# Moving the low part of the inner features from VectorE to GpSimd in the seven-product pairs of a SwiGLU kernel

## The chip, the cores and the metric

The kernel runs on one core of one Trainium2 chip. The metric is the device time of one launch in microseconds, the median of several runs. TensorE (PE) does matmuls, VectorE (DVE) and ScalarE (ACT) elementwise work, GpSimd (POOL) here a few sums and some transfers, SyncE (SP) issues the weight loads.

## The reference, cut to what matters

The program is one step of a two-layer decoder trunk on 512 prompt positions and 32 sample positions (544 columns in all), width 1024. It has four SwiGLU channel mixers (FFNs), each with 2816 inner features:

```
def swiglu(x, w13, w2):
    gate, up = jnp.split(x @ w13, 2, axis=-1)
    return (jax.nn.silu(gate) * up) @ w2

x = layer_norm(ALPHA * x + 0.5 * swiglu(x, ffn_w13[layer, 0], ffn_w2[layer, 0]), ...)
x = layer_norm(ALPHA * x + mix, ...)            # pooling or dilated attention
x = layer_norm(ALPHA * x + 0.5 * swiglu(x, ffn_w13[layer, 1], ffn_w2[layer, 1]), ...)
```

Everything is in fp32. Each matmul is done in a faster format by splitting both factors into a high part (rounded to fp32r) and a low part (the rest), and adding three products: high x high, high x low, low x high.

## The kernel before, in words

Activations lie with features on the 128 partitions and the 544 columns along the free axis. An FFN's 2816 inner features are 22 units of 128; eleven of them are made in stage `up<f>a` and used in `down<f>a`, the other eleven in `up<f>b` and `down<f>b` (f is 0 to 3). The first units of an a stage (6 in `up0a`, 4 in each of the others, table `PLAIN`) are made plainly. The rest, 5, 7, 7 and 7 units of the a stages and all 11 of each b stage, 70 in all, are made as "seven-product pairs": gate and up product of one unit are computed together from seven products of quarter matrices, after sums and differences of the weight quarters. A pair is 7 x 12 = 84 matmuls on TensorE.

What follows is what each engine does for one pair `i`, in the order of its program; the order is written out by hand in one function `pair` per engine.

- SP (`stream_seven`) loads four quarters of the raw weights of the next unit, each when the piece of `raw` has been read: quarters 0 and 2 first, quarter 1, and quarter 3 last, once `seven_low(5)` has read the old one.
- ACT (`pair`, L1444) rounds the seven weight quarters or sums (`seven_high`, tiles `t_a_hi`, `t_s_hi`, `t_w_seven`), takes the silu in two halves, copies one product (`t_p`), and rounds the finished features of the unit before (`hidden_hi`, tile `t_h_hi`, L1412).
- DVE (`pair`, L1947) makes the sums of the weight quarters for the next unit (`w_sums`, tile `t_w_sum`, L1922), the low parts of the seven (`seven_low`, L1927), combines the products (`added`, tiles `t_u` and `t_c`, L1931), multiplies silu and up part into `hf` in two halves (`hidden_seven`, L1943), and makes the low part of the features of the unit before: `hidden_lo`, L1873 to L1877, tile `t_h_lo`, hf minus its rounded part, 128 x 544.
- PE (`pair`, L881) does product 0 to 6. Product 6 adds to the bank from which DVE has just made `c22`, so it waits for that (`pe.wait_ge(c_made, 5 * y + 3)`).

`hf` is one buffer: `hidden_seven(stage, i, 0)` waits for `h_lo_made` of the unit before. PE waits for `h_lo_made` once more: in the first turn of `down`, which follows the last pair, for the last but one unit at k = 0 and for the last unit at k = 10 of 11 (`each`, L961).

GpSimd in this kernel: after each FFN and mixer, `sums` (L2439, tensor_tensor adds of 128 x 544, L2449 and L2451, beside a stage whose DVE work is `residual` and `round_lo`, L1805) and `centre` (L2457, L2463, 128 x 272), between `down2b` and `wo` the loads of the caches and small copies. In the FFNs before `down<f>b` it waits.

Of the kernel before, what the change touches and what calls it, by code (L numbers as in the profile page):

```python
# [24 lines left out]
F32 = mybir.dt.float32  # L25
F32R = mybir.dt.float32r
ACT = mybir.ActivationFunctionType
ALU = mybir.AluOpType
# [45 lines left out]
PLAIN = {"up0a": 6, "up1a": 4, "up2a": 4, "up3a": 4, "up0b": 0, "up1b": 0, "up2b": 0, "up3b": 0}  # L74
# [19 lines left out]
UNITS = {n: u for n, u, _ in STAGES}  # L94
# [9 lines left out]
HIDDEN = {n: FC * int(n[2]) + (KH if n[3] == "b" else 0) for n in PLAIN}  # L104
# [51 lines left out]
def first_turn(i):  # L156
    return isinstance(i, int) and i == 0
# [26 lines left out]
def build(nc, A, O):  # L184
# [3 lines left out]
    def sb(where, name, shape, dt=F32):  # L188
        return where.enter_context(nc.sbuf_tensor("t_" + name, shape, dt))

    def sem(name):
        return ctx.enter_context(nc.semaphore(name))

    with ctx:
# [23 lines left out]
        sg, hf, sq = (elem[:, j * T:(j + 1) * T] for j in range(3))  # L218
# [35 lines left out]
        hhi = sb(rh, "h_hi", [P, KH, T], F32R)  # L254
        hlo = sb(rh, "h_lo", [P, KH, T], F32R)
# [99 lines left out]
        def hcols(j):  # L355
            return slice(j * HALF, (j + 1) * HALF)
# [57 lines left out]
        h_hi_made = sem("hidden_hi_made")  # L414
        h_lo_made = sem("hidden_lo_made")
# [1373 lines left out]
        def _(dve):  # L1789
# [57 lines left out]
            n = NBUCKET + 1  # L1847
# [25 lines left out]
            def hidden_lo(stage, i):  # L1873
                dve.wait_ge(h_hi_made, HIDDEN[stage] + i + 1)
                one = lambda t: t.rearrange("p (a n) -> p a n", a=1)
                nc.vector.tensor_tensor(hlo[:, bass.ds(i, 1), :], one(hf[:]), hhi[:, bass.ds(i, 1), :].bitcast(F32),
                                        ALU.subtract).then_inc(h_lo_made, 1)  # L1877
# [27 lines left out]
            def w_sums(y, m):  # L1905
                if m == 0:
                    dve.wait_ge(quarter_in[3], 16 * (y + 1))
                    a, b, op = quarter(2), quarter(3), ALU.add
                elif m == 1:
                    dve.wait_ge(w_sum_made, 4 * y + 2)  # L1910
                    a, b, op = w_sum[0][:], quarter(0), ALU.subtract
                elif m == 2:
                    dve.wait_ge(quarter_in[0], 16 * (y + 1))
                    dve.wait_ge(quarter_in[2], 16 * (y + 1))
                    if not (isinstance(y, int) and y == 0):
                        dve.wait_ge(seven_lo_made, 7 * y - 3)
                    a, b, op = quarter(0), quarter(2), ALU.subtract
                else:
                    dve.wait_ge(quarter_in[1], 16 * (y + 1))
                    dve.wait_ge(w_sum_made, 4 * y + 3)  # L1920
                    a, b, op = quarter(1), w_sum[1][:], ALU.subtract
                nc.vector.tensor_tensor(w_sum[m][:], a, b, op).then_inc(w_sum_made, 1)  # L1922

            def seven_low(n, y):
                src = (quarter(0), w_sum[1][:], w_sum[0][:], w_sum[2][:], quarter(1), quarter(3), w_sum[3][:])[n]
                dve.wait_ge(seven_hi_made, 7 * y + n + 1)
                nc.vector.tensor_tensor(seven_lo[n][:], src, seven_hi[n][:].bitcast(F32), ALU.subtract) \  # L1927
                    .then_inc(seven_lo_made, 1)

            def added(out, a, b):  # L1930
                nc.vector.tensor_tensor(out[:], a, b[:], ALU.add).then_inc(c_made, 1)  # L1931

            def c_last(y, odd):
                dve.wait_ge(seven_done, 7 * y + 7)
                added(c12, pb[:, odd, 0:HALF], u2)

            def hidden_seven(stage, i, half):
                y = SEVEN[stage] + i - PLAIN[stage]
                dve.wait_ge(seven_silu, 2 * y + 1 + half)
                if half == 0:  # L1940
                    dve.wait_ge(h_lo_made, HIDDEN[stage] + i)
                    dve.wait_ge(c_made, 5 * y + 4)
                m = nc.vector.tensor_tensor(hf[:, hcols(half)], sg[:, hcols(half)], (c21, c22)[half][:], ALU.mult)  # L1943
                if half:
                    m.then_inc(h_made, 1)

            def pair(stage, i, odd):  # L1947
                y = SEVEN[stage] + i - PLAIN[stage]
                first = isinstance(i, int) and i == PLAIN[stage]
                last = isinstance(i, int) and i == UNITS[stage] - 1  # L1950
                if not first:
                    c_last(y - 1, 1 - odd)
                seven_low(6, y)
                if not first:
                    hidden_seven(stage, i - 1, 1)
                if not last:
                    seven_low(0, y + 1)
                if not first:
                    hidden_lo(stage, i - 1)
                if not last:  # L1960
                    w_sums(y + 1, 2)
                    w_sums(y + 1, 0)
                dve.wait_ge(p1_copied, y + 1)
                dve.wait_ge(seven_done, 7 * y + 2)
                added(u2, pc[:, 0, 0:HALF], p1)
                if not last:
                    w_sums(y + 1, 1)
                    w_sums(y + 1, 3)
                    seven_low(1, y + 1)
                    seven_low(2, y + 1)  # L1970
                dve.wait_ge(seven_done, 7 * y + 4)
                dve.wait_ge(c_made, 5 * y + 1)
                added(u3, pc[:, 1, 0:HALF], u2)
                dve.wait_ge(c_made, 5 * y + 2)
                added(c22, pb[:, odd, 0:HALF], u3)
                if not last:
                    seven_low(3, y + 1)
                    seven_low(4, y + 1)
                if last:
                    round_lo(AFTER[stage], 0, 0)  # L1980
                dve.wait_ge(seven_done, 7 * y + 6)
                added(c21, pd[:, 0, 0:HALF], u3)
                hidden_seven(stage, i, 0)
                if not last:
                    seven_low(5, y + 1)
                    return
                c_last(y, odd)
                hidden_seven(stage, i, 1)
                round_lo(AFTER[stage], 1, 0)
                hidden_lo(stage, i)  # L1990

            def pairs(stage):
                n = PLAIN[stage]
# [442 lines left out]

        @block.gpsimd
        def _(pool):
            def sums(stage):  # L2439

                pool.wait_ge(res_made, RBASE[stage] + 1)
                nc.gpsimd.memset(accs[:], 0.0).then_inc(acc_zero, 1)  # L2442
                nc.gpsimd.memset(accq[:], 0.0).then_inc(acc_zero, 1)
                pool.wait_ge(acc_zero, 2 * RES.index(stage) + 2)
                def add(c):
                    if not first_turn(c):
                        pool.wait_ge(acc_made, ABASE[stage] + 2 * c)
                    pool.wait_ge(res_made, RBASE[stage] + c + 1)
                    nc.gpsimd.tensor_tensor(accs[:], accs[:], x[:, c, :], ALU.add).then_inc(acc_made, 1)  # L2449
                    pool.wait_ge(sq_made, RBASE[stage] + c + 1)  # L2450
                    nc.gpsimd.tensor_tensor(accq[:], accq[:], sq[:], ALU.add).then_inc(acc_made, 1)  # L2451

                add(0)
                with pool.Fori(1, DC - 2) as c:
                    add(c)

            def centre(stage):  # L2457

                n = RES.index(stage)
                for j in range(2):  # L2460
                    pool.wait_ge(ln_std, 2 * n + j + 1)
                    for c in range(5, DC):
                        nc.gpsimd.tensor_tensor(x[:, c, hcols(j)], x[:, c, hcols(j)], mean[:, hcols(j)], ALU.subtract) \  # L2463
                            .then_inc(ln_sub, 1)

            sums("down0b")
            centre("down0b")

            pool.wait_ge(utok_ok, 1)
            pool.dma_start(O["pool_p"][0, 0, :, :], utok[0:PAD, :]).then_inc(utok_out, 16)  # L2470
            pool.dma_start(O["pool_s"][0, :, PAD - DEC_S:PAD, :], utok[PAD:PAD + SAMP, :]).then_inc(utok_out, 16)
            sums("pout")
            centre("pout")
            sums("down1b")
            centre("down1b")

            sums("down2b")
            centre("down2b")

# [80 lines left out]
            pool.wait_ge(o_ready, GC)  # L2560
            sums("wo")
            centre("wo")
            sums("down3b")
            centre("down3b")

# [22 lines left out]
```

## Time and profile before

| | us |
|---|---|
| median of 3 runs (lowest, highest) | 2268.6 (2266.86, 2274.68) |
| the profiled execution | 2272.91 |
| its span | 2271.2 |
| TensorE busy in the span | 2154.2 (95%) |
| VectorE busy | 1443.8 (64%) |
| ScalarE busy | 867.1 (38%) |
| GpSimd busy | 224.5 (10%) |

The span runs from the first to the last instruction; the 1.7 us between it and the execution's own time are around it. Busy shares are averages over stages of very different kinds, and matmuls overlap one another, so that a gap of under 0.16 us between two matmul starts doesn't show as idle time of TensorE. For a stage, the starts of instructions in a timeline tell more.

### The profile page before, as it was taken

The numbers are of one execution on the slowest core, as the hardware profiler recorded it, in microseconds if no ns is written. First come the engines' busy times: TensorE is split into PE (matmuls) and PEld (weight loads), VectorE is DVE, ScalarE is ACT, GpSimd is POOL, SyncE is SP. The second block draws the span as 40 slices with busy tenths as digits, with TensorE's granted clock in tenths as the row PEclk, the third lists the DMA queues.
The fourth block names the chain that finished last, engine by engine and source line by source line (L and its number), as shares of the span: only waits on it lengthen the run. The fifth ranks groups of instructions, "written<-read, shape, count | busy, mean of one in ns | idle before, by whom it ended". The sixth has DMA issues, their size and how long they took to land.

```text
span 2271.2 us, 44028 instructions
## 1 busy us (share of the span) xinstructions
PE 2154.2 (95%) x16591; PEld 2056.9 (91%) x16591; DVE 1443.8 (64%) x2474; ACT 867.1 (38%) x1521; POOL 224.5 (10%) x240
## 2 busy tenths in 40 slices
PE   7999999979999999999999999989889988999998
PEld 7899999969999999999999999988856688999997
DVE  3582894684894696479469652467444376937955
ACT  3341453442552344355235434222222345514533
POOL 0000002204000001300000130210020040000022
PEclk9999999989999999999999999999877889999998
DMA  4242433212233233234333324666663322333331
GB/s 136 73 132 85 128 112 103 67 52 80 76 100 94 86 93 101 76 95 142 102 94 97 100 79 156 210 211 214 200 209 115 111 75 70 92 95 89 95 106 53
DMA packets 381501, 249.78 MB, mean 110 GB/s; under 512 B 10423, under 2 KB 363039, under 8 KB 381327
## 3 DMA queue, kind: packets, MB, share of 16 engines
q1 hardware_dynamic: 371271, 210.00, 31.2%
q0 software_dynamic: 10096, 37.94, 4.8%
q8 instruction: 91, 1.49, 0.3%
q14 instruction: 43, 0.34, 0.1%
HBM read 230.63 MB, written 22.35 MB: 111 GB/s over the span
## 4 chain that ended last, share of the span: by engine, by line
PE 74%; DVE 11%; DMA 6%; issue 4%; ACT 3%; SPq 1%; POOL 1%; DVEq 0%; ACTq 0%; POOLq 0%
PE pair L748 33%; PE pair L877 25%; PE pair L787 5%; DMA t_w_raw<-in_attn_w_kv 3%; PE pair L1005 2%; DMA t_w_raw<-in_ffn_w 2%; PE pair L1239 2%; DVE t_w_seven L1927 2%; PE pair L1156 1%; DVE t_w_sum L1922 1%; PE pair L1262 1%; PE pair L760 1%; DVE t_w_lo L1805 1%; ACT t_w_hi L1362 1%; DVE t_u_sum L2214 1%
## 5 line engine op out<-in xcount | busy, mean ns | idle before, releaser
L877 PE MATMUL pair<-t_x_diff_hi,t_w_seven 128*128 128x272 f32 x1960 | 410.0, 290 | 0.0
L1362 ACT ACTIVATE t_w_hi<-t_w_raw 128x1024 fp32r<-128x1024 f32 (+2 forms) x152 | 177.1, 1170 | 465.0 <-PE pair L748 389.8
L1805 DVE TENSOR_TENSOR t_w_lo<-t_w_raw,t_w_hi 128x1024 fp32r<-128x1024 f32 (+2 forms) x152 | 232.6, 1531 | 190.9 <-ACT t_w_hi L1362 185.4
L877 PEld LDWEIGHTS pair<-t_x_diff_hi,t_w_seven 128*128 128x128 f32 x1960 | 320.6, 188 | 0.0
L748 PE MATMUL pair<-t_h_lo,t_w_hi 128*128 128x272 f32 x1232 | 255.2, 288 | 0.0
L748 PE MATMUL pair<-t_h_hi,t_w_lo 128*128 128x272 f32 x1232 | 255.0, 288 | 0.0
L877 PE MATMUL pair<-t_x_hi,t_w_seven 128*128 128x272 f32 x1120 | 240.9, 295 | 14.8 <-DVE t_c L1931 13.2
L748 PE MATMUL pair<-t_h_hi,t_w_hi 128*128 128x272 f32 x1232 | 254.8, 288 | 0.0
L877 PE MATMUL pair<-t_x_diff_lo,t_w_seven 128*128 128x272 f32 x840 | 241.9, 288 | 0.0
L877 PEld LDWEIGHTS pair<-t_x_hi,t_w_seven 128*128 128x128 f32 x1120 | 184.6, 188 | 27.1 <-issue 12.8
L748 PEld LDWEIGHTS pair<-t_h_hi,t_w_lo 128*128 128x128 f32 x1232 | 193.2, 188 | 0.0
L748 PEld LDWEIGHTS pair<-t_h_hi,t_w_hi 128*128 128x128 f32 x1232 | 193.2, 188 | 0.0
L748 PEld LDWEIGHTS pair<-t_h_lo,t_w_hi 128*128 128x128 f32 x1232 | 193.1, 188 | 0.0
L1433 ACT ACTIVATE t_w_seven<-t_w_sum 128x512 fp32r<-128x512 f32 x210 | 124.6, 622 | 113.0 <-PE pair L877 79.6
L877 PE MATMUL pair<-t_x_lo,t_w_seven 128*128 128x272 f32 x560 | 161.8, 289 | 0.0
L877 PEld LDWEIGHTS pair<-t_x_diff_lo,t_w_seven 128*128 128x128 f32 x840 | 158.7, 189 | 0.0
L1927 DVE TENSOR_TENSOR t_w_seven<-t_w_sum,t_w_seven 128x512 fp32r<-128x512 f32 x210 | 143.5, 683 | 0.2
L748 PE MATMUL pair<-t_x_hi,t_w_hi 128*128 128x272 f32 x576 | 124.2, 298 | 20.3 <-DVE t_w_lo L1805 15.7
L2442 POOL MEMSET t_work<- 128x544 f32 x6 | 3.3, 553 | 1403.1 <-DVE t_stream L2075 1403.1
L1433 ACT ACTIVATE t_s_hi<-t_w_sum 128x512 fp32r<-128x512 f32 x70 | 44.3, 633 | 247.3 <-DVE t_w_sum L1922 222.9
L748 PE MATMUL pair<-t_x_lo,t_w_hi 128*128 128x272 f32 x576 | 122.6, 295 | 0.0
L748 PE MATMUL pair<-t_x_hi,t_w_lo 128*128 128x272 f32 x576 | 122.4, 295 | 0.0
(308 smaller groups left out, 5046.3 us busy)
## 6 DMA issues: line engine op xcount, KB each, us to landing
t_w_raw<-in_ffn_w SPq DMA_DIRECT2D x280, 256.0 KB, 3.1
t_w_raw<-in_ffn_w SPq DMA_DIRECT2D x64, 704.0 KB, 4.5
t_w_raw<-in_ffn_w SPq DMA_DIRECT2D x36, 512.0 KB, 3.8
t_cached<-in_cache_kv_w POOLq DMA_DIRECT2D x16, 1024.0 KB, 9.0
t_cached_v<-in_cache_kv_w POOLq DMA_DIRECT2D x16, 1024.0 KB, 10.3
t_w_raw<-in_attn_w_kv SPq DMA_DIRECT2D x24, 512.0 KB, 8.0
t_w_raw<-in_attn_w_q SPq DMA_DIRECT2D x12, 512.0 KB, 3.8
scratch_bias_rows<-scratch_bias_row SPq DMA_DIRECT2D x12, 384.0 KB
```

Source lines behind the costliest of these rows:

```text
L748: m = nc.tensor.matmul(out[:, j, 0:HALF], w[:, at + k, :], a(k)[:, j * HALF:(j + 1) * HALF], start=first and k == 0 and n == 0, stop=last ...
L760: return nc.tensor.matmul(out[:, j, 0:HALF], invd[:], a[:, hcols(j)], start=first, stop=not first)
L787: m = nc.tensor.matmul(ps[2 * u + s][:, j, 0:HALF], w[:, k, :], a[:, k, hcols(j)], start=k == 0 and n == 0, stop=k == DC - 1 and n == 2)
L877: m = nc.tensor.matmul(out[:, 0:HALF], w[:, k, :], b, start=start and k == 0 and j == 0, stop=k == 3 and j == 2, skip_group_check=not start)
L1005: m = nc.tensor.matmul(ps[s][:, j, 0:HALF], w[:, k, :], a(k)[:, hcols(j)], start=k == 0 and n == 0, stop=k == KT[stage] - 1 and n == 2)
L1156: nc.tensor.matmul(out[:, (g + 1) * P:(g + 2) * P], q_r[hd, g * GC + c, :], k_r[hd, (g - 1) * GC + c, :], start=True, stop=True)
L1239: m = nc.tensor.matmul(pd[32 * s:32 * s + 32, 0, :], p_b[s][:, t, :], v_c0[s][:] if t == 0 else v_c[s][:, t - 1, :], start=t == 0, stop=t ...
L1262: m = nc.tensor.transpose(pb[:, h % 2, k * P:(k + 1) * P], p_p[h % 2][:, k * P:(k + 1) * P], ident[:])
L1362: nc.scalar.activation(whi[s][:, 0:KT[stage], :], raw[s][:, 0:KT[stage], :], ACT.Copy) \
L1433: nc.scalar.activation(seven_hi[n][:], src, ACT.Copy).then_inc(seven_hi_made, 1)
L1805: nc.vector.tensor_tensor(wlo[s][:, 0:k, :], raw[s][:, 0:k, :], whi[s][:, 0:k, :].bitcast(F32), ALU.subtract).then_inc(lo_made[s], 1)
L1927: nc.vector.tensor_tensor(seven_lo[n][:], src, seven_hi[n][:].bitcast(F32), ALU.subtract) \
```

## The change

For the 70 seven-product pairs `hidden_lo` is made by GpSimd. It has a loop for each of the eight up stages, placed in its program ahead of the sums of that FFN. Each turn waits until ACT has rounded unit i, subtracts, and raises `h_lo_made` as DVE did. DVE drops the instruction and its wait from `pair`; it still makes `hidden_lo` for the 18 plain units.

```
@@ DVE, pair
                 if not last:
                     seven_low(0, y + 1)
-                if not first:
-                    hidden_lo(stage, i - 1)
                 if not last:
                     w_sums(y + 1, 2)
                     w_sums(y + 1, 0)
...
                 hidden_seven(stage, i, 1)
                 round_lo(AFTER[stage], 1, 0)
-                hidden_lo(stage, i)
@@ GpSimd
+            def hidden_lo(stage):
+                one = hf[:].rearrange("p (a n) -> p a n", a=1)
+                with pool.Fori(PLAIN[stage], UNITS[stage]) as i:
+                    pool.wait_ge(h_hi_made, HIDDEN[stage] + i + 1)
+                    nc.gpsimd.tensor_tensor(hlo[:, bass.ds(i, 1), :], one, hhi[:, bass.ds(i, 1), :].bitcast(F32),
+                                            ALU.subtract).then_inc(h_lo_made, 1)
...
+            hidden_lo("up0a")
+            hidden_lo("up0b")
             sums("down0b")
             centre("down0b")
```

The same two calls stand ahead of `sums("down1b")`, `sums("down2b")` and `sums("down3b")`.

On DVE, in the loop of the pairs, these rows stood from the low part of quarter a11 to the second sum (`t_a_lo` is `seven_low(0)`, `t_w_sum` are `w_sums` 2 and 0, `t_u` the first addition of products):

```order
L1927 TENSOR_TENSOR t_a_lo<-t_w_raw,t_a_hi 128x512 [waits seven_hi_made]
L1874 REGISTER_ALU
L1876 ISA [waits hidden_hi_made]
L1876 TENSOR_TENSOR t_h_lo<-t_elementwise,t_h_hi 128x544
L1913 ISA
L1916 REGISTER_ALU [waits w_quarter_in2,w_quarter_in0]
L1922 TENSOR_TENSOR t_w_sum<-t_w_raw 128x512 [waits seven_lo_made]
L1922 TENSOR_TENSOR t_w_sum<-t_w_raw 128x512 [waits w_quarter_in3]
```

and now:

```order
L1927 TENSOR_TENSOR t_a_lo<-t_w_raw,t_a_hi 128x512 [waits seven_hi_made]
L1913 ISA
L1916 REGISTER_ALU [waits w_quarter_in2,w_quarter_in0]
L1922 TENSOR_TENSOR t_w_sum<-t_w_raw 128x512 [waits seven_lo_made]
L1922 TENSOR_TENSOR t_w_sum<-t_w_raw 128x512 [waits w_quarter_in3]
L1962 REGISTER_ALU [waits p1_copied]
L1931 TENSOR_TENSOR t_u<-pair,t_p 128x272 [waits seven_products]
```

The subtraction and its wait for ACT are gone, and the two sums stand directly behind `t_a_lo`.

GpSimd's program now begins, behind its constants, with the loops of `up0a` and `up0b`:

```order
L2438 UNCONDITIONAL_BRANCH
L2438 ISA
L2440 ISA [waits hidden_hi_made]
L2440 ISA
L2440 TENSOR_TENSOR t_h_lo<-t_elementwise,t_h_hi 128x544
L2438 REGISTER_ALU
L2438 COMPARE_AND_BRANCH
```

One wait and one subtraction per turn; before, the first rows behind the constants were the memsets of `sums("down0b")`. The rows of PE and ACT are the same in both kernels.

## Rows read from the trace of the kernel before

**Rows 1.** The page's busy time, share of the span and instructions of each engine.

```profile
PE 2154.2 (95%) x16591; PEld 2056.9 (91%) x16591; DVE 1443.8 (64%) x2474; ACT 867.1 (38%) x1521; POOL 224.5 (10%) x240
```

**Rows 2.** Engines' busy time in stretches of pairs; columns in the first line.

```profile
core 0: us, PE busy (x) PEld busy (x) DVE busy (x) ACT busy (x) POOL busy (x), PEclk, DMA share, GB/s
268.47:333.62 65.15, 64.95 (x507) 63.69 (x505) 61.48 (x115) 33.78 (x66) 0.00 (x0) 1.00 0.39 116
...
635.33:645.97 10.64, 10.64 (x86) 10.61 (x85) 10.16 (x19) 5.54 (x11) 0.00 (x0) 1.00 0.35 101
```

**Rows 3.** Timeline of PE around product 6; start, length, what.

```profile
310.00 0.29 PE L877 MATMUL pair<-t_x_diff_hi,t_w_seven 128*128 128x272 f32 x1
310.32 0.39 PE L877 MATMUL pair<-t_x_hi,t_w_seven 128*128 128x272 f32 x1
310.55 0.29 PE L877 MATMUL pair<-t_x_lo,t_w_seven 128*128 128x272 f32 x1
```

**Rows 4.** Timeline of DVE in that pair; in brackets idle time and who ended it.

```profile
303.44 0.69 DVE L1927 TENSOR_TENSOR t_a_lo<-t_w_raw,t_a_hi 128x512 fp32r<-128x512 f32 x1 [0.18 <-ACT t_a_hi L1433]
304.42 0.73 DVE L1876 TENSOR_TENSOR t_h_lo<-t_elementwise,t_h_hi 128x544 f32 x1 [0.29 <-ACT t_h_hi L1412]
305.06 1.29 DVE L1922 TENSOR_TENSOR t_w_sum<-t_w_raw 128x512 f32<-128x512 f32 x2
306.26 0.43 DVE L1931 TENSOR_TENSOR t_u<-pair,t_p 128x272 f32<-128x272 f32 x1
...
309.75 0.44 DVE L1931 TENSOR_TENSOR t_c<-pair,t_u 128x272 f32<-128x272 f32 x1
```

**Rows 5.** Timeline of ACT in that pair.

```profile
303.58 0.65 ACT L1412 ACTIVATE t_h_hi<-t_elementwise 128x544 f32 x1
```

**Rows 6.** The load of quarter 3 in that pair: SP's timeline, then the DMA view.

```profile
302.12 0.37 SPq L572 DMA_DIRECT2D t_w_raw<-in_ffn_w  x1
...
t_w_raw<-in_ffn_w SPq DMA_DIRECT2D x1, 256.0 KB, 3.0
```

**Rows 7.** Timeline of POOL, then of DVE, in `down0b`.

```profile
381.14 1.36 POOL L2449 TENSOR_TENSOR t_work<-t_work,t_stream 128x544 f32<-128x544 f32 x1 [4.37 <-DVE t_stream L2075]
382.45 2.75 POOL L2451 TENSOR_TENSOR t_work<-t_work,t_elementwise 128x544 f32<-128x544 f32 x1
...
381.52 2.46 DVE L1805 TENSOR_TENSOR t_w_lo<-t_w_raw,t_w_hi 128x1408 fp32r<-128x1408 f32 x1 [0.56 <-ACT t_w_hi L1362]
```

**Rows 8.** Timeline of POOL, then of DVE, in a `centre`.

```profile
434.54 1.83 POOL L2463 TENSOR_TENSOR t_stream<-t_stream,t_work 128x272 f32<-128x272 f32 x1 [13.65 <-ACT t_work L1561]
...
434.52 1.22 DVE L1802 TENSOR_TENSOR t_w_lo_second<-t_w_raw,t_w_hi_second 128x1024 fp32r<-128x1024 f32 x1
435.65 1.85 DVE L2125 RECIPROCAL t_work<-t_work 128x272 f32<-128x272 f32 x1
```

**Rows 9.** POOL, whole run: `centre` in ns min/median/max; a group with a cast.

```profile
L2463 POOL TENSOR_TENSOR t_stream<-t_stream,t_work x36: 755/772/1835, 418.6 to 2258.1; 128x272 f32<-128x272 f32 x36
L2498 POOL CAST t_one_hot<-t_ident_twice 64x512 fp32r (+1 forms) x8 | 4.9, 608 | 116.6 <-DVE t_k_times_q L2270 116.5
```

**Rows 10.** Timeline of DVE in the second pair of `up0b`.

```profile
249.04 0.69 DVE L1927 TENSOR_TENSOR t_a_lo<-t_w_raw,t_a_hi 128x512 fp32r<-128x512 f32 x1 [0.68 <-ACT t_a_hi L1433]
249.88 0.73 DVE L1876 TENSOR_TENSOR t_h_lo<-t_elementwise,t_h_hi 128x544 fp32r<-128x544 f32 x1
```

**Rows 11.** Timeline of DVE in a pair of `up1b`.

```profile
805.18 0.69 DVE L1922 TENSOR_TENSOR t_w_sum<-t_w_raw 128x512 f32<-128x512 f32 x1
806.32 0.69 DVE L1922 TENSOR_TENSOR t_w_sum<-t_w_raw 128x512 f32<-128x512 f32 x1 [0.44 <-DMA t_w_raw<-in_ffn_w]
```

**Rows 12.** End of `up0b`: timeline of DVE, then the chain that ended last.

```profile
356.54 1.62 DVE L1805 TENSOR_TENSOR t_w_lo<-t_w_raw,t_w_hi 128x1408 fp32r<-128x1408 f32 x1
358.07 0.72 DVE L1876 TENSOR_TENSOR t_h_lo<-t_elementwise,t_h_hi 128x544 fp32r<-128x544 f32 x1
...
355.20 49.77 PE pair L748 x396
```

More of the change, by code:

```diff
@@ L1957, in pair @@
                     seven_low(0, y + 1)
-                if not first:
-                    hidden_lo(stage, i - 1)
                 if not last:
@@ L1989, in pair @@
                 round_lo(AFTER[stage], 1, 0)
-                hidden_lo(stage, i)
             def pairs(stage):
@@ L2438, in _, with hidden_lo @@
         def _(pool):
+            def hidden_lo(stage):
+                one = hf[:].rearrange("p (a n) -> p a n", a=1)
+                with pool.Fori(PLAIN[stage], UNITS[stage]) as i:
+                    pool.wait_ge(h_hi_made, HIDDEN[stage] + i + 1)
+                    nc.gpsimd.tensor_tensor(hlo[:, bass.ds(i, 1), :], one, hhi[:, bass.ds(i, 1), :].bitcast(F32),
+                                            ALU.subtract).then_inc(h_lo_made, 1)
             def sums(stage):
@@ L2464, in centre @@
                             .then_inc(ln_sub, 1)
+            hidden_lo("up0a")
+            hidden_lo("up0b")
             sums("down0b")
@@ L2473, in _ @@
             centre("pout")
+            hidden_lo("up1a")
+            hidden_lo("up1b")
             sums("down1b")
             centre("down1b")
+            hidden_lo("up2a")
+            hidden_lo("up2b")
             sums("down2b")
@@ L2562, in _ @@
             centre("wo")
+            hidden_lo("up3a")
+            hidden_lo("up3b")
             sums("down3b")
```

## The prediction

> **What bounds the kernel now.** The page comes first. TensorE is busy 95% of the span, VectorE 64%, GpSimd 10% [rows 1]. That average says that DVE has room, and it is the wrong place to stop, because the change touches only the seven-product pairs. So the next view is the busy time by stretch, laid over the pairs. Six pairs of `up0b` take 65.15 us, 10.86 each, and in them DVE is busy 61.48, 10.25 per pair [rows 2]: 94%, not 64%. PE shows 64.95 busy in the same stretch, but its matmuls overlap, so I ask the timeline for their starts. They come every 0.12 to 0.13 us, except at product 6: 310.00 to 310.32, then 310.55 [rows 3], that is 0.19 + 0.10 = 0.29 us lost. Product 6 waits for `c22`, and DVE ends that `t_c` at 309.75 + 0.44 = 310.19 [rows 4]. So in these pairs PE waits for DVE, hidden below the threshold at which idle time shows. What PE could do without this: a pair that lost almost nothing took 10.64 [rows 2], and 396 matmuls of a down stage took 49.77 us, 0.1257 each, which gives 84 x 0.1257 = 10.56 for a pair [rows 12]. PE's floor is then 10.56 to 10.64, and 0.22 to 0.30 us per pair could be had from a faster DVE.
>
> In one turn DVE waits for no matmul. It runs from sum to sum, and waits only for ACT: 0.18 before `t_a_lo` and 0.29 before `t_h_lo` [rows 4]. Hence DVE's own chain of instructions is the period of the pair, and whatever it gains or loses, the pair gains or loses, down to PE's floor.
>
> **How many pairs.** There are 70. In the first pair of each of the 8 stages nothing was moved, and the last pair is treated below. 70 - 16 = 54 pairs are left.
>
> **What the change removes from DVE.** `t_a_lo` starts at 303.44 and is followed by a 0.69 us instruction; behind such a one the next starts 0.60 later (two `t_w_sum` take 1.29, so the second starts 0.60 after the first [rows 4]). Without `t_h_lo` the first sum can start at 304.04 in place of 305.06: 1.02 us earlier, 0.64 of it the instruction and 0.38 the wait for ACT.
>
> **What it adds.** On its own engine, nothing that matters: GpSimd is idle here, its subtraction of 128 x 544 should take what its additions of that size take when nothing disturbs them, 1.36 us [rows 7], and `hf` is needed again only by `hidden_seven`, which stands behind `c22` (309.75 [rows 4]), over 5 us later. The question is what it does to DVE. In `down0b` the two engines meet [rows 7]. DVE's `t_w_lo` of 1408 columns starts at 381.52 while GpSimd's first addition runs to 382.50, and takes 2.46 us in place of 1.62 (its length undisturbed [rows 12]). It ends at 383.98 as if it had begun at 382.36, 0.14 before GpSimd's end. GpSimd's second addition, issued at 382.45, takes 2.75 in place of 1.36: it ends at 385.20, 1.22 after DVE's end. So each of the two waits for the other's whole instruction when both read two operands from SBUF. `centre` says the same: GpSimd's instruction of 272 columns takes 0.77 as a rule [rows 9], and 1.83 when it meets a 1.22 us one of DVE [rows 8]; it ends at 436.37, 0.63 after DVE's 435.74, and 0.77 - 0.14 is 0.63. The reciprocal behind it, with one operand, starts at 435.65 while GpSimd works and takes its 1.85 [rows 8].
>
> Now the same in a pair. ACT ends `t_h_hi` at 303.58 + 0.65 = 304.23 [rows 5]. DVE took 0.19 from there to start [rows 4], so I let GpSimd ask at 304.42. DVE is then in its first sum, 304.04 to 304.73, two operands from SBUF: GpSimd waits. The second sum could start at 304.64, but it needs quarter 3, whose load was issued at 302.12 and takes 3.0 to land [rows 6], 305.1. So nobody contests GpSimd's turn. It ends at 304.73 + 1.22 = 305.95, and DVE's second sum begins in effect at 305.95 - 0.14 = 305.81. Before, it began at 305.06 + 0.60 = 305.66. **The pair becomes 0.15 longer, not shorter**: 1.02 us are taken off DVE, the early quarter is not there to use them, and the port costs 1.17 from the end of the first sum (1.22 - 0.14 + the 0.09 by which two instructions overlap). Both engines' orders behind it are unchanged, so the shift runs through to `c22` and PE. The same reckoning on the other steady pairs gives 0.15 to 0.17; I take 0.16.
>
> Seven pairs, the second of a stage, differ: there `t_h_lo` follows `t_a_lo` by 0.84 in place of 0.98 [rows 10], since ACT was early. Less wait is removed, and they lose 0.30 each. In three pairs the second sum waited for its quarter well past the subtraction (805.18 + 0.60 = 805.78, started 806.32 [rows 11]); GpSimd's turn fits into that wait but for some 0.04.
>
> Sum: 44 x 0.16 + 7 x 0.30 + 3 x 0.04 = 7.0 + 2.1 + 0.1 = **9.2 us slower**.
>
> **Costed at nothing.** The last pair: PE's first down turn asks for the last unit's `t_h_lo` at k = 10, after 60 matmuls, 355.20 + 7.5 = 362.7. GpSimd asks at about 357.5, waits for `t_w_lo` (to 358.16 [rows 12]) and ends 1.22 later, 359.4. The cover is 3.3 us; if GpSimd needed more, PE would wait at 8 places. The other `t_h_lo` of the last pair lies beside DVE's wait for PE. The loops stand ahead of `sums`, which can't start before the down stage has its first result; no transfer of GpSimd is passed.
>
> **Bounds of the unknown.** No row has a GpSimd two-operand instruction that writes fp32r. From below: if its output cost nothing and it were no obstacle at all, DVE would gain 0.46 (the sum at 305.2, when the quarter lands) and PE's floor caps that at 0.28, 54 x 0.28 = 15 us gained. From above: add a whole cast to fp32r, 0.61 [rows 9]: 54 x 0.61 = 33 more. I take the plain 1.36, the nearest row.
>
> The Trainium skill, GPSIMD Engine Reference, § Performance versus the Vector engine, gives 4497 ns for a two-input add of 2048 fp32 columns. By length alone that is an estimate of 1.19 us for 544 columns; the sum would be 54 x 0.17 lower, 0 in place of 9. The trace has 1.36 for this size and that is what I use.
>
> **The rivals.**
> 1. *PE becomes the bound* (faster). If GpSimd gets its operands beside DVE's instructions, or in DVE's pauses, DVE's chain falls below PE's floor and each pair takes 10.58: -15 us, 2254. The reciprocal above was not held up, and `t_u`, 128 x 272, reads only one operand from SBUF: a turn of GpSimd that began under it would hide 0.36 us of its hold. Against it: GpSimd asks before the first sum ends, and the turn then falls at once. The Trainium skill, SBUF — State Buffer, § Who interferes with whom, has the rule: a DVE instruction with at most one SBUF input doesn't contend, one with two does. By that rule the sums contend, and the trace agrees with 2.46 in place of 1.62.
> 2. *A draw.* Turns shorter by 0.1 to 0.2 than the additions', or a part of the gained 1.02 kept elsewhere (ACT's `t_s_hi`, the loads): the two sides cancel, 0 to +5, about 2271.
> 3. *A dearer turn.* The fp32r output makes the instruction 0.3 longer, or DVE and GpSimd meet twice in a pair: +0.3 x 54 = 16 on top of 9, 2294.
> 4. *It doesn't do what it says*: GpSimd's loops would have to be late for `hidden_seven`. With 5 us to spare I give that no chance of its own.
>
> **How the numbers follow.** The profiled execution took 2272.9 in all (span 2271.2); with 9.2 it would take 2282.1. It lies 4.3 above the median of the runs shown, and the same 9.2 on 2268.6 gives 2277.8, so 2278. Chances: forecast 0.62, rival 1 0.12, rival 2 0.13, rival 3 0.13. 0.3% (what a measurement can tell from no change) is 6.8 us. The forecast's own range is +6 to +13, and I give a tenth of it to "same": slower 0.56 + 0.13 = 0.69, same 0.19, faster 0.12. The range leaves out rival 1's centre and the far half of rival 3: 2263 to 2290.
>
> **What would show it.** `t_h_lo` on GpSimd at about 1.5 us each in the pairs (1.36 and a short wait). In a steady pair DVE's second sum should be recorded with some 1.3 us in place of 0.69, all other DVE instructions unchanged. Six pairs in place of 65.15 should take 66.1, and the gap before product 6 should grow by 0.16. Down stages, norms and attention must be unchanged to 1 us in all. I am wrong if the pairs take 10.6 (no lock), if a sum shows 0.69 beside a running GpSimd instruction, or if the turn is much over 1.5 us.

## The result and the profile after

The changed kernel takes 2277.18 us (median of 20 runs, 2268.65 to 2287.23), the kernel before 2267.3 (20 runs, 2259.01 to 2276.48). The ratio is 1.0039, with a 95% interval of 1.0027 to 1.0051: 8.8 us slower, between 6.1 and 11.6. Forecast were 9.2.

The profiled executions alone would mislead: the span after is 2267.1 us, 4.1 shorter than before's 2271.2. So the first thing to do is to cut both at the pairs. These are the stretches of before, then of after, up to the first pair of `up0a`, and from the last pair of `up2b` to the first of `up3a` (columns as in [rows 2]):

```profile
0.00:111.61 111.61, 97.16 (x656) 90.97 (x656) 48.45 (x66) 34.81 (x45) 0.20 (x4) 0.95 0.36 102
1268.83:1914.67 645.84, 599.01 (x4671) 532.36 (x4669) 333.68 (x606) 212.50 (x389) 104.47 (x154) 0.90 0.47 150
```

```profile
0.00:107.02 107.02, 92.90 (x655) 87.65 (x656) 48.36 (x66) 34.84 (x45) 0.20 (x4) 0.98 0.36 106
1268.25:1908.85 640.60, 596.45 (x4671) 529.74 (x4669) 332.54 (x604) 212.70 (x389) 107.86 (x156) 0.91 0.47 151
```

4.6 and 5.2 us were gained, the first where no instruction was changed, the second where only the two subtractions at the last pair of `up2b` were moved. The column PEclk, the share of full speed that TensorE was granted, differs in both: 0.95 and 0.98 in the first stretch, 0.90 and 0.91 in the second. Length times missing share gives, as an estimate, 5.6 us lost to the clock in the first stretch before and 2.1 after, so most of the 4.6. The runs of one kernel scatter by more than this (2259 to 2276), which is why 20 runs of each are compared. In the pairs, where the granted clock is 1.00 in every stretch of both kernels, the picture is another. This is the sum row over eight stretches, each from the second pair of a stage to its last, 54 pairs, of before and then of after:

```profile
sum 589.66, PE 583.93 PEld 573.37 DVE 554.18 ACT 302.56 POOL 0.00; mean PE 72.99 PEld 71.67 DVE 69.27 ACT 37.82 POOL 0.00
```

```profile
sum 596.92, PE 584.78 PEld 573.32 DVE 553.12 ACT 302.46 POOL 82.35; mean PE 73.10 PEld 71.66 DVE 69.14 ACT 37.81 POOL 10.29
```

7.3 us longer. TensorE's and ScalarE's busy time stayed. DVE's fell by only 1.1, although 54 instructions of 0.73 were taken from it: most of that came back as longer instructions, for a held instruction is recorded with its wait. The steady pairs, answering to [rows 2]:

```profile
264.11:330.22 66.11, 64.97 (x506) 63.70 (x505) 62.07 (x109) 33.77 (x66) 9.17 (x6) 1.00 0.38 115
632.06:642.99 10.93, 10.83 (x86) 10.61 (x85) 10.12 (x18) 5.53 (x11) 1.50 (x1) 1.00 0.35 99
```

Six pairs take 66.11 in place of 65.15, and the second pair of `up1a` 10.93 in place of 10.64. In the timelines of DVE and of POOL, answering to [rows 4], one sees where:

```profile
299.52 0.69 DVE L1927 TENSOR_TENSOR t_a_lo<-t_w_raw,t_a_hi 128x512 fp32r<-128x512 f32 x1 [0.16 <-ACT t_a_hi L1433]
300.13 0.68 DVE L1922 TENSOR_TENSOR t_w_sum<-t_w_raw 128x512 f32<-128x512 f32 x1
301.31 1.28 DVE L1922 TENSOR_TENSOR t_w_sum<-t_w_raw 128x512 f32<-128x512 f32 x1 [0.49 <-DMA t_w_raw<-in_ffn_w]
302.51 0.43 DVE L1931 TENSOR_TENSOR t_u<-pair,t_p 128x272 f32<-128x272 f32 x1
```

```profile
300.51 1.53 POOL L2440 TENSOR_TENSOR t_h_lo<-t_elementwise,t_h_hi 128x544 f32 x1 [9.48 <-ACT t_h_hi L1412]
```

GpSimd asks at 300.51 while the first sum runs to 300.81, ends at 302.04, 1.23 after it, and the second sum takes 1.28 in place of 0.69: its end, 302.59, is that of an instruction begun at 301.90, 0.14 before GpSimd's. Part of the hold lies under the 0.49 us in which DVE waits for quarter 3 anyway. Product 6 then waits longer than in [rows 3], 0.48 from one start to the next in place of 0.32:

```profile
306.09 0.29 PE L877 MATMUL pair<-t_x_diff_hi,t_w_seven 128*128 128x272 f32 x1
306.57 0.39 PE L877 MATMUL pair<-t_x_hi,t_w_seven 128*128 128x272 f32 x1 [0.19 <-DVE t_c L1931]
306.80 0.29 PE L877 MATMUL pair<-t_x_lo,t_w_seven 128*128 128x272 f32 x1
```

### The profile page after: what moved, and what is told of

The parts are those of the page before. It is cut to its first block, busy times and chain, and to the rows that moved or that the text cites. A ratio compares the mean times of both kernels' runs of the same rounds, so it can differ in the third digit from the quotient of the medians.

```text
span 2267.1 us, 44233 instructions
## 1 busy us (share of the span) xinstructions
PE 2147.8 (95%) x16591; PEld 2049.9 (90%) x16591; DVE 1432.9 (63%) x2404; ACT 867.4 (38%) x1521; POOL 332.8 (15%) x310
## 4 chain that ended last, share of the span: by engine, by line
PE 62%; DVE 16%; DMA 9%; issue 7%; ACT 3%; SPq 1%; POOL 1%; DVEq 0%; ACTq 0%; POOLq 0%
PE pair L748 33%; PE pair L877 13%; DMA t_w_raw<-in_ffn_w 6%; PE pair L787 5%; DVE t_w_seven L1927 4%; DMA t_w_raw<-in_attn_w_kv 3%; PE pair L1005 2%; PE pair L1239 2%; DVE t_w_sum L1922 2%; DVE t_u L1931 2%; DVE t_c L1931 1%; PE pair L1156 1%; PE pair L1262 1%; PE pair L760 1%; DVE t_w_lo L1805 1%
## 5 line engine op out<-in xcount | busy, mean ns | idle before, releaser
L2440 POOL TENSOR_TENSOR t_h_lo<-t_elementwise,t_h_hi 128x544 f32 x70 | 108.1, 1544 | 1195.2 <-ACT t_h_hi L1412 1195.2
L1922 DVE TENSOR_TENSOR t_w_sum<-t_w_raw 128x512 f32<-128x512 f32 x140 | 129.6, 928 | 57.8 <-DMA t_w_raw<-in_ffn_w 57.8
```

The lines of the kernel that those rows point to most:

```text
L2440: nc.gpsimd.tensor_tensor(hlo[:, bass.ds(i, 1), :], one, hhi[:, bass.ds(i, 1), :].bitcast(F32), ALU.subtract).then_inc(h_lo_made, 1)
```

## The experiments

The edits are shown against the changed kernel where nothing else is said. Each ratio is against runs of the kernel before that were made beside it: 25 runs with a median of 2267.57 us for the first four experiments, 21 runs with 2265.39 for the other four. "54 pairs" is the sum over the same eight stretches as above, 589.66 before. The theory under test is that of the prediction: an instruction of DVE and one of GpSimd that read through the same port wait for each other's full length, and what that costs depends on what DVE has to do just then. The rivals are that DVE's removed microsecond was of no use to begin with, and that GpSimd's turn has a fixed price wherever it stands.

**Take the reading away.** The subtraction becomes a memset, so the low part of these features is left out.

```
-                with pool.Fori(PLAIN[stage], UNITS[stage]) as i:
+                for i in range(PLAIN[stage], UNITS[stage]):
                     pool.wait_ge(h_hi_made, HIDDEN[stage] + i + 1)
-                    nc.gpsimd.tensor_tensor(hlo[...], one, hhi[...].bitcast(F32), ALU.subtract).then_inc(h_lo_made, 1)
+                    nc.gpsimd.memset(hlo[:, bass.ds(i, 1), :].bitcast(F32), 0.0).then_inc(h_lo_made, 1)
```

> GpSimd's 70 subtractions of the pairs are replaced by memsets of 128x544 that write zeros into t_h_lo and read nothing; the low part of those features is left out of the result. DVE's program is that of the changed kernel. Theory (each engine waits for the other's whole instruction when both read two operands from SBUF): DVE's second t_w_sum is no longer held (0.69 us, not 1.3) and starts when quarter 3 lands, about 0.46 us earlier than in the kernel before; DVE's chain falls under PE's floor, a steady pair takes 10.56 to 10.64 in place of 10.86, and the whole is 12 to 15 us faster than before (ratio 0.9935 to 0.995). Rival A (DVE's removed microsecond is not usable at all, because the quarters or ACT set the chain): pairs stay at 10.86, ratio 1.000. Rival B (the price of GpSimd's turn is its semaphores and its start, not the port): pairs stay at 11.02, ratio 1.004.

Measured: ratio 0.9938 (0.9921 to 0.9956), 14 us faster than before (9 runs). DVE and POOL in a pair of `up1a`:

```profile
667.63 0.69 DVE L1927 TENSOR_TENSOR t_a_lo<-t_w_raw,t_a_hi 128x512 fp32r<-128x512 f32 x1 [0.46 <-ACT t_a_hi L1433]
668.24 1.29 DVE L1922 TENSOR_TENSOR t_w_sum<-t_w_raw 128x512 f32<-128x512 f32 x2
```

```profile
668.48 0.55 POOL L2440 MEMSET t_h_lo<- 128x544 f32 x1 [10.01 <-ACT t_h_hi L1412]
```

Two sums in 1.29 us as before, with a memset of GpSimd running beside them; all 70 memsets take 0.551 to 0.557. The pairs of this stage take 10.57, PE's floor: the stretch of five reads

```profile
633.56:686.39 52.83, 52.83 (x422) 52.83 (x421) 49.03 (x92) 28.38 (x55) 2.77 (x5) 1.00 0.31 91
```

Rivals A and B both fall: the microsecond is usable (54 pairs in 575.22), and neither the semaphores nor the start of GpSimd's instruction is what costs. One detail was not as expected. DVE's second sum doesn't stand at the landing of the quarter here. Once PE is the bound, DVE waits earlier (0.46 us before `t_a_lo`), and the quarter has landed by then.

**Two halves, each where it is covered.** Nothing is left out.

```
+                def turn(i, placed):
                     pool.wait_ge(h_hi_made, HIDDEN[stage] + i + 1)
...
+                    half(0, h_lo_half)
+                    pool.wait_ge(h_lo_half, SEVEN[stage] + i - PLAIN[stage] + 1)
+                    if placed:
+                        pool.wait_ge(seven_lo_made, 7 * (SEVEN[stage] + i - PLAIN[stage] + 2) + 2)
+                    half(1, h_lo_made)
```

`half(j, ...)` is the same subtraction on half `j` of the columns, 0 to 271 or 272 to 543; `placed` is false for the last two units of a stage.

> Nothing is left out. GpSimd makes t_h_lo in two halves of 128x272: the first as soon as ACT has rounded the unit, the second when DVE has made the second low part of the next pair (seven_lo_made), so that it lies under t_u and t_c, which have only one operand in SBUF; in the last two units of a stage it doesn't wait. Theory (the port is held for the instruction's length, and only against DVE instructions with two SBUF operands): the first half asks at 304.4, runs from the end of the first t_w_sum (304.73) to 305.36 and is out of the way at 305.22, just when quarter 3 has landed (305.1 to 305.2); the second is held from 309.4 to 309.9 under 0.82 us of t_u and t_c. Both are free, a steady pair takes PE's 10.56 to 10.64, 12 to 15 us faster than before (ratio 0.9935 to 0.995). Rival (a GpSimd instruction costs DVE a fixed price wherever it stands): two instructions per pair cost at least what one did, 11.02 or more per pair, ratio 1.004 or more.

Measured: ratio 0.996 (0.9943 to 0.9977), 9 us faster (9 runs), 54 pairs in 577.81. The second half, DVE and then POOL:

```profile
666.68 0.68 DVE L1928 TENSOR_TENSOR t_w_seven<-t_w_sum,t_w_seven 128x512 fp32r<-128x512 f32 x1
667.28 0.43 DVE L1932 TENSOR_TENSOR t_u<-pair,t_u 128x272 f32<-128x272 f32 x1
667.74 0.44 DVE L1932 TENSOR_TENSOR t_c<-pair,t_u 128x272 f32<-128x272 f32 x1
668.10 0.68 DVE L1928 TENSOR_TENSOR t_w_seven<-t_w_sum,t_w_seven 128x512 fp32r<-128x512 f32 x1
```

```profile
666.95 1.05 POOL L2442 TENSOR_TENSOR t_h_lo<-t_elementwise,t_h_hi 128x272 f32 x1 [3.16 <-DVE t_w_seven L1928]
```

GpSimd waits for the low part (ends 667.36) and is done at 668.00. `t_u` and `t_c`, whose other operand comes from PSUM, run beside it at their usual length, and the next low part, begun at 668.10, is not held. The fixed-price rival, 1.004 or more, falls. The first half is not free of DVE as expected: in the next pair of `up1a` it asks at 673.41, and the second sum, ready at 673.95, takes 0.95 in place of 0.69. That costs nothing where PE is the bound. The pairs of `up1a` stand at 10.57, but those in the first part of `up0b` do not, and the whole fell short of the 12 to 15 us: see the experiment with the bias pieces.

**One instruction, later.** The whole subtraction, behind the same wait for DVE.

```
+                def turn(i, placed):
                     pool.wait_ge(h_hi_made, HIDDEN[stage] + i + 1)
+                    if placed:
+                        pool.wait_ge(seven_lo_made, 7 * (SEVEN[stage] + i - PLAIN[stage] + 2) + 2)
                     nc.gpsimd.tensor_tensor(hlo[...], one, hhi[...].bitcast(F32), ALU.subtract).then_inc(h_lo_made, 1)
```

> Nothing is left out. GpSimd makes t_h_lo in one instruction of 128x544, but only when DVE has made the second low part of the next pair, so that it begins under t_u and t_c. Theory: 1.17 us of hold less the 0.82 us of t_u and t_c leave 0.35 for the next low part (recorded near 1.0 us in place of 0.68); the second t_w_sum comes 0.46 us earlier than before. Net 0.11 us less per pair than before: 10.75, and 6 us faster in all (ratio 0.997). Rival (position doesn't matter, only the amount): 11.02 per pair, ratio 1.004.

Measured: ratio 0.9975 (0.996 to 0.9989), 5.7 us faster (12 runs); the median of the 54 pair periods is 10.70. The low part behind `t_c` is held, DVE then POOL:

```profile
668.88 0.44 DVE L1932 TENSOR_TENSOR t_c<-pair,t_u 128x272 f32<-128x272 f32 x1
669.24 1.03 DVE L1928 TENSOR_TENSOR t_w_seven<-t_w_sum,t_w_seven 128x512 fp32r<-128x512 f32 x1
```

```profile
668.08 1.63 POOL L2443 TENSOR_TENSOR t_h_lo<-t_elementwise,t_h_hi 128x544 f32 x1 [9.09 <-DVE t_w_seven L1928]
```

1.03 against 0.68, that is the 0.35 expected. It is the same in all eight stages: beside GpSimd's subtraction all 54 `t_u` take 0.43 and all 54 `t_c` 0.44, and the low part behind them 1.01 to 1.04. The rival that these two are spared for being short (272 columns), and not for their operand in PSUM, doesn't fit another row: in the changed kernel DVE's `t_stream` of 128 x 544, which also reads PSUM, runs from 1821.15 to 1821.87 beside two additions of GpSimd (1820.12 to 1821.47, 1821.44 to 1822.80), takes its usual 0.72 and holds neither. The same instruction, elsewhere, turns 8.8 us of loss into 5.7 of gain: place decides, not amount.

**Twice.** GpSimd subtracts twice for every unit.

```
-                with pool.Fori(PLAIN[stage], UNITS[stage]) as i:
+                for i in range(PLAIN[stage], UNITS[stage]):
                     pool.wait_ge(h_hi_made, HIDDEN[stage] + i + 1)
+                    nc.gpsimd.tensor_tensor(hlo[...], one, hhi[...].bitcast(F32), ALU.subtract).then_inc(h_lo_half, 1)
+                    pool.wait_ge(h_lo_half, SEVEN[stage] + i - PLAIN[stage] + 1)
                     nc.gpsimd.tensor_tensor(hlo[...], one, hhi[...].bitcast(F32), ALU.subtract).then_inc(h_lo_made, 1)
```

> GpSimd subtracts twice for every unit of a pair, one after the other; the result is unchanged. Theory: the second turn asks at 306.2, during DVE's second t_w_sum (ends 306.5), and ends at 307.7; 0.36 of its hold lies under t_u, so the third t_w_sum is held by some 0.8 us. Steady pair 11.8, the whole 9 + 54 x 0.8 = 52 us slower than before (ratio 1.023). If only the quarter's wait made the first turn costly, or DVE had slack left, the second would cost little: under 0.3 per pair, ratio under 1.011.

Measured: ratio 1.024 (1.021 to 1.0269), 54 us slower (two runs). DVE, then POOL:

```profile
310.20 0.43 DVE L1932 TENSOR_TENSOR t_u<-pair,t_p 128x272 f32<-128x272 f32 x1
310.55 1.50 DVE L1923 TENSOR_TENSOR t_w_sum<-t_w_sum,t_w_raw 128x512 f32<-128x512 f32 x1
```

```profile
309.81 1.69 POOL L2444 TENSOR_TENSOR t_h_lo<-t_elementwise,t_h_hi 128x544 fp32r<-128x544 f32 x1
```

The third sum is held by 1.50 - 0.68 = 0.82, and the pairs take 71.04 / 6 = 11.84:

```profile
269.32:340.36 71.04, 64.97 (x507) 63.70 (x505) 66.83 (x109) 33.09 (x66) 20.02 (x12) 1.00 0.35 106
```

DVE has no slack in a pair of this kernel: the hold of 0.82 comes back whole in the period, 11.84 against 11.02.

**One operand on GpSimd.** A copy of `hf` in place of the subtraction, so the low part of these features is not made.

```
-                    nc.gpsimd.tensor_tensor(hlo[...], one, hhi[...].bitcast(F32), ALU.subtract).then_inc(h_lo_made, 1)
+                    nc.gpsimd.tensor_copy(hlo[:, bass.ds(i, 1), :], one).then_inc(h_lo_made, 1)
```

> GpSimd's subtraction is replaced by a copy of hf (128x544) into t_h_lo, one operand read from SBUF; so the low part is wrong in the result. Theory in its strict form (GpSimd's reads go through the port that DVE's second operand needs): the copy, alone some 0.65 us (a cast of 64x512 took 0.61), asks at 304.4 while DVE's first t_w_sum runs to 304.73, waits for it, is recorded with about 0.8 and is over by 305.3, under the wait for quarter 3; pairs take 10.57 as with the memset and the ratio is 0.994. Rival (only two-operand instructions of GpSimd take part): it is recorded with its own length in every pair, none longer by 0.1 or more; the pairs are the same.

Measured: ratio 0.9945 (0.9927 to 0.9962), 12.5 us faster (two runs). DVE, then POOL:

```profile
665.24 1.73 DVE L1922 TENSOR_TENSOR t_w_sum<-t_w_raw 128x512 f32<-128x512 f32 x2
```

```profile
665.59 0.84 POOL L2440 CAST t_h_lo<-t_elementwise 128x544 f32 x1 [9.73 <-ACT t_h_hi L1412]
```

The copy's shortest record in the run is 0.643; here it takes 0.84, because it waits for the first sum, and the two sums take 1.73 in place of 1.29. So a GpSimd instruction with one operand takes part too, and the rival falls. The total doesn't show it, since these pairs are bound by PE. One step was off: the copy was to be over before quarter 3 lands, but here the second sum is held by 0.44.

**Only the last unit of a stage on GpSimd.** One part of the change alone.

```
@@ DVE, pair
+                if not first:
+                    hidden_lo(stage, i - 1)
@@ GpSimd
-                with pool.Fori(PLAIN[stage], UNITS[stage]) as i:
+                for i in (UNITS[stage] - 1,):
```

> DVE makes t_h_lo in all pairs as before, and GpSimd only that of the last unit of each stage (8 in place of 70 instructions). Theory: its turn ends some 3 us before PE needs it, and nothing changes: steady pairs 10.86, ratio 1.000 within 0.002. Rival (part of the loss is at the ends of the stages, where PE or the next stage's DVE work waits for GpSimd): ratio 1.002 or more, and PE shows a gap at k = 10 of the first down turn.

Measured: ratio 1.0004 (0.9988 to 1.002; 10 runs). The ends of the stages cost nothing that this resolves, as forecast. In `down0b` GpSimd's turn ends at 355.27, PE asks for its result some 60 matmuls behind 350.94, at about 358.5, and its matmuls go on there at 0.125 us each, without a gap. The 54 pairs, whose program is that of before, summed to 588.42 in this execution, 1.2 less than before's 589.66, so such a sum scatters by at least that. One pair makes up 0.74 of it: the fourth of `up3a`, in which DVE waits for a weight quarter, took 12.24 before and 11.50 here, and 11.50 to 12.46 over all ten traces.

**The pieces of the bias table moved.** Against the kernel with the placed halves: SP sends the pieces elsewhere.

```
-            stream_all("down0a")
-            for i in range(7):
-                stream_seven("up0b", i)
+            for i in range(4):
+                stream("down0a", i)
                 bias_piece(1 if i < 3 else 2, (i + 1) % 4)
-            stream_all("up0b", 7)
+            stream_all("up0b")
...
+            for i in range(4):
+                stream("down0b", i)
+                if i < 3:
+                    bias_piece(2, i + 1)
```

> The kernel with two placed halves, and the seven pieces of the bias table (384 KB each) that SP sends during the first seven pairs of up0b are sent during down0a (4) and down0b (3). Nothing is left out. Theory: in up0b the pairs that stay at 10.86 with the halves and with the memset are bound by the landing of the weight quarters beside these pieces, not by DVE; they now take 10.57 like the others, 7 x 0.29 = 2 us less, and the down stages have room for the pieces (5.6 MB in 66 us). Ratio to before 0.994. Rival (these pairs are slow for another reason, a chain of DVE and ACT that starts late in this stage): they stay at 10.86 and the ratio at 0.996.

Measured: ratio 0.9944 (0.9925 to 0.9963), 12.7 us faster than before (6 runs), the lowest ratio of the versions that leave nothing out. The nine middle pairs of `up0b`, with the halves alone and then with the pieces moved:

```profile
243.68:341.36 97.68, 96.67 (x758) 95.39 (x757) 88.78 (x163) 51.10 (x99) 17.83 (x18) 1.00 0.39 117
```

```profile
245.78:340.88 95.10, 95.10 (x758) 95.10 (x757) 88.91 (x163) 51.74 (x99) 17.89 (x18) 1.00 0.33 98
```

95.10 / 9 = 10.57, 2.6 us less in this stage, where 2 were expected: most of these pairs had been held by the landing of the weight quarters. With the halves alone ACT waited 3.2 us in all, in six of them, for the quarter of `t_a_hi` to land; with the pieces moved it never does. That its total differs from the halves' by more than chance can't be said from the intervals (0.9943 to 0.9977 against 0.9925 to 0.9963); the pair periods say it.

**Halves back to back.** Against the kernel with the placed halves: the second half no longer waits for DVE's low part.

```
                 with pool.Fori(PLAIN[stage], UNITS[stage] - 2) as i:
-                    turn(i, True)
+                    turn(i, False)
```

> Two halves of 128x272 on GpSimd, the second directly behind the first, with no wait for DVE's low part. Nothing is left out. Theory: the first is out of the way when quarter 3 lands; DVE's second t_w_sum runs 305.2 to 305.9; the second half asks during it, begins at its end under t_u and holds the third t_w_sum by some 0.2 us. DVE's chain is 0.46 - 0.2 = 0.25 shorter than before, 10.6: pairs at 10.57 to 10.65, ratio 0.994 to 0.996. Rival (two halves back to back cost what the whole does): 11.02, ratio 1.004.

Measured: ratio 0.9971 (0.996 to 0.9982), 6.6 us faster (8 runs), a steady pair 10.67. DVE, then POOL:

```profile
301.09 0.96 DVE L1923 TENSOR_TENSOR t_w_sum<-t_w_raw 128x512 f32<-128x512 f32 x1 [0.22 <-DMA t_w_raw<-in_ffn_w]
301.97 0.43 DVE L1932 TENSOR_TENSOR t_u<-pair,t_p 128x272 f32<-128x272 f32 x1
302.32 0.91 DVE L1923 TENSOR_TENSOR t_w_sum<-t_w_sum,t_w_raw 128x512 f32<-128x512 f32 x1
```

```profile
300.56 0.94 POOL L2442 TENSOR_TENSOR t_h_lo<-t_elementwise,t_h_hi 128x272 f32 x1 [8.76 <-ACT t_h_hi L1413]
301.69 1.00 POOL L2442 TENSOR_TENSOR t_h_lo<-t_elementwise,t_h_hi 128x272 f32 x1 [0.19 <-POOL t_h_lo L2442]
```

The third sum is held by 0.91 - 0.68 = 0.23, where 0.2 was expected. The steady pairs lie just above what was told (10.57 to 10.65), the ratio a little outside it (0.994 to 0.996), in part for `up0b`, whose fourth to seventh pair take 10.82 to 10.89 here too.

## Why the prediction was right

- *What bounds the pairs.* That PE waits for DVE's chain was right and is now shown from both sides: a shorter chain gave 10.57 per pair, a longer one 11.84. For the first part of `up0b` it was incomplete. There the quarters land beside the pieces of the bias table, and with the shorter chains (halves, memset, copy) its fourth to seventh pair still take 10.81 to 10.94, 10.88 in the mean. I chose my six steady pairs from this stage, and that the two limits agree there, 10.88 and 10.86, was luck.
- *The removed microsecond.* Right in the changed kernel: the first sum starts 0.61 behind `t_a_lo`, and DVE then waits 0.49 us for quarter 3, as the landing at 305.1 had said [rows 6].
- *The price of a turn.* Taken from [rows 7, 8], where it had been recorded between other instructions. GpSimd ended 1.23 after the first sum (told: 1.22), the held sum in effect 0.14 before that (told: 0.14). Steady pairs +0.16 (66.11 - 65.15 = 0.96 for six), and the second pair of `up1a` +0.29 for 0.30.
- *The sum.* 9.2 told, 7.3 found in the 54 pairs of one execution each, with a scatter of at least 1.2, and 8.8 (6.1 to 11.6) by the clock of the runs. Pair by pair, from one first matmul to the next, the differences fall into three groups. 42 pairs grew by 0.12 to 0.19, 6.9 us together: the 0.16 told. Five of the eight second pairs grew by 0.26 to 0.30. The other seven pairs, which had taken 10.95 to 12.24 before, changed by -0.59 to +0.10, 1.05 us less together. The -0.59 is the fourth pair of `up3a`, whose length scatters by itself. The term that was too large is the one of the seven second pairs: those of `up0a`, `up0b` and `up2b` changed by +0.10, -0.12 and -0.01, not by 0.30. In that of `up0b`, from which the term was taken [rows 10], DVE's stretch from `t_a_lo` to the end of the second sum did grow, from 2.77 to 3.07, but a wait for the load ahead of it went away. ACT's rows for the quarter before `t_a_lo`, before and after:

```profile
248.38 0.63 ACT L1433 ACTIVATE t_a_hi<-t_w_raw 128x512 fp32r<-128x512 f32 x1 [0.50 <-DMA t_w_raw<-in_ffn_w]
```

```profile
243.84 0.64 ACT L1433 ACTIVATE t_a_hi<-t_w_raw 128x512 fp32r<-128x512 f32 x1
```

  That the same holds for the pairs of `up0a` and `up2b` is argued. That the total of the runs came so near to 9.2 is partly luck: the interval of 6.1 to 11.6 holds the 7.3 as well.
- *Costed at nothing.* The last pair: borne out by the run with only the last units on GpSimd, within its interval. The unknown fp32r output: GpSimd's shortest `t_h_lo` is 1.360 us, the additions' 1.36, so no cost shows, and rival 3 fell.
- *The draw*, which an estimate from the figure of the Trainium skill, GPSIMD Engine Reference, § Performance versus the Vector engine, would have given (1.19 us per turn), didn't come: the shortest turn has the 1.36 us of the trace.
- *PE becomes the bound* (rival 1): false for this kernel, but exactly what happens when the turn is halved and placed. What I didn't see while weighing it is that it could be had by asking later.

## What to carry to other kernels

Before an instruction goes from VectorE to GpSimd, look at the operands of the VectorE instructions that will run beside it. In the rows of this case, those with two operands in SBUF and a GpSimd instruction that reads SBUF waited for each other in full. So the move paid only where it was put, if need be in pieces, beside instructions that read PSUM, or into a wait that was there anyway. And read the starts of the matmuls, not their busy time: 0.29 us in every pair of a TensorE that looked 99.7% busy here were worth 12.7 us with nothing left out. The weight loads' busy time (PEld) shows most of it: 63.69 of 65.15 us in [rows 2], 0.24 idle per pair, against 95.10 of 95.10 in the pairs bound by TensorE.

## What the runs showed of the hardware beyond what was expected

- A GpSimd copy with a single SBUF operand meets VectorE's two-operand instructions in the same way: 0.84 in place of 0.64 us, and the sums beside it 1.73 in place of 1.29. A memset, which reads nothing, kept its 0.55 and held neither sum. The Trainium skill, SBUF — State Buffer, § Who interferes with whom, says the same of an instruction that only writes; the trace agrees with 1.29 us for the two sums beside the memset.
- Writing fp32r showed no cost on GpSimd: the subtraction of 128 x 544 took 1.348 to 1.360 us at its shortest in the changed kernel, the late and the doubled one, and the two additions with fp32 output 1.339 and 1.351 in the kernel before.
- With one piece of 384 KB sent beside the 1 MB of weights of a pair, the fourth to seventh pair of `up0b` took 10.81 to 10.94 us where PE alone needs 10.57.
- A held instruction is recorded with the wait inside its length: 1.28 for a sum of 0.69, 1.53 for a subtraction of 1.36.
